# mLSTM and DSA stages of a three-block transformer kernel: score multiplies one step later, normalizations in pairs, mask and bias table summed on GpSimd

## The reference, cut to what matters

```python
# mLSTM, per head (the kernel does all 256 rows at once, the factors as one matrix exp(D))
s = einsum('blhd,bshd->bhls', q_, k_) * exp(D - m_t[..., None])
den = s.sum(-1) + ...
den = maximum(abs(den), exp(-m_t))
h = num / den.transpose(0, 2, 1)[..., None]
# DSA, per head
bias = rel_bias[t5_bucket(max(t - idx, 0))]
logits = (qb @ k_sel) * dh ** -0.5 + bias
logits = where(valid, logits, -inf)          # only the top-k keys of the indexer
probs = softmax(logits); out = probs @ v_sel
```

## Time and profile before

| | us |
|---|---|
| median of 3 runs | 882.55 (880.82 to 882.99) |
| the profiled execution | 882.83 |
| its span | 881.0 |
| granted clock of TensorE, mean | 0.996 of 2.4 GHz |

### The profile page before, as it was taken

How to read it: one execution, slowest core, us unless ns; L and a number is a source line. 1 busy time by engine, 2 the same in 40 slices (tenths; PEclk the granted TensorE clock), 3 DMA queues, 4 the chain that set the end, 5 groups by cost and what they waited for, 6 DMA issues and landing times. The chain is left out here.

```text
span 881.0 us, 14633 instructions
## 1 busy us (share of the span) xinstructions
PE 856.0 (97%) x5810; PEld 754.6 (86%) x5810; DVE 668.0 (76%) x1096; ACT 458.7 (52%) x737; POOL 66.2 (8%) x61
## 2 busy tenths in 40 slices
PE   9999989999999999999999999999999999999996
PEld 9989978767876888699999999679987899999995
DVE  6698798869977996799757857796777876556567
ACT  5564555454556645475454545265564854454450
POOL 1100001000001120011210100110000111001011
PEclk9999999999999999999999999999999999999999
DMA  9856576556965870799866897379617986645501
GB/s 344 298 178 200 191 245 226 191 157 206 337 238 206 276 272 1 304 371 374 288 221 218 290 342 251 118 242 351 226 50 277 330 294 203 210 153 196 187 1 48
DMA packets 56916, 200.67 MB, mean 228 GB/s; under 512 B 6600, under 2 KB 7936, under 8 KB 56848
## 3 DMA queue, kind: packets, MB, share of 16 engines
q1 hardware_dynamic: 55808, 196.50, 63.6%
q0 software_dynamic: 1040, 3.24, 1.2%
HBM read 198.57 MB, written 1.08 MB: 227 GB/s over the span
## 5 line engine op out<-in xcount | busy, mean ns | idle before, releaser
L1230 PE MATMUL ps<-XT,wsp 128*128 128x256 f32 x760 | 215.5, 283 | 2.2 <-DVE wsp L1471 1.3
L1231 PE MATMUL ps<-XT,wsp 128*128 128x256 f32 x760 | 212.5, 280 | 0.0
L1232 PE MATMUL ps<-XT,wsp 128*128 128x256 f32 x760 | 212.3, 279 | 0.0
L1471 DVE TENSOR_TENSOR wsp<-ring,wsp 128x1024 fp32r<-128x1024 f32 x140 | 173.5, 1248 | 7.5 <-ACT wsp L2047 7.3
L2047 ACT CAST wsp<-ring 128x1024 fp32r<-128x1024 f32 x140 | 145.5, 1046 | 61.6 <-PE ps L1232 52.8
L1230 PEld LDWEIGHTS ps<-XT,wsp 128*128 128x128 f32 x760 | 142.9, 188 | 5.9 <-issue 2.9
L1231 PEld LDWEIGHTS ps<-XT,wsp 128*128 128x128 f32 x760 | 142.8, 188 | 0.5
L1232 PEld LDWEIGHTS ps<-XT,wsp 128*128 128x128 f32 x760 | 142.7, 188 | 0.0
L1230 PE MATMUL ps<-wsp,ra 128*128 128x512 f32 (+1 forms) x256 | 97.6, 381 | 2.5 <-DVE ra L1508 1.1
L1232 PE MATMUL ps<-wsp,ra 128*128 128x512 f32 (+1 forms) x256 | 96.9, 379 | 0.0
L1231 PE MATMUL ps<-wsp,ra 128*128 128x512 f32 (+1 forms) x256 | 96.8, 378 | 0.0
(11 more groups left out here) (278 smaller groups left out, 1538.6 us busy)
## 6 DMA issues: line engine op xcount, KB each, us to landing
arena<-in_mod_w SPq DMA_DIRECT2D x48, 512.0 KB, 6.1
ring<-in_mod_w SPq DMA_DIRECT2D x44, 512.0 KB, 4.8
ring<-in_ffn_a SPq DMA_DIRECT2D x28, 512.0 KB, 5.0
ring<-in_ffn_b SPq DMA_DIRECT2D x28, 512.0 KB, 5.0
arena<-in_ffn_o SPq DMA_DIRECT2D x22, 512.0 KB, 4.7
ring<-in_ffn_o SPq DMA_DIRECT2D x22, 512.0 KB, 4.8
arena<-in_ffn_a SPq DMA_DIRECT2D x16, 512.0 KB, 5.4
arena<-in_ffn_b SPq DMA_DIRECT2D x16, 512.0 KB, 4.8
```

Of the source, the lines that this page charges most:

```text
L1230: pe.matmul(o, l[0], r[0], start=start, stop=False)
L1231: pe.matmul(o, l[0], r[1], start=False, stop=False)
L1232: return pe.matmul(o, l[1], r[0], start=False, stop=stop)
L1471: ve.tensor_tensor(w[:, 1024:1024 + n], raw[slot[0]][:, 0:n], w[:, 0:n].bitcast(f32), SUB).then_inc(*done("V", "lo", u, also=[("raw", *slo ...
```

## The change

- In `mlstm`, the second operation of a score tile becomes a step of its own, `ml_x`, queued one step of the mLSTM later: after `ml_s` of the next tile, and ahead of `ml_o`. The banks are given back there.
- The denominators: ScalarE takes Abs of the last column for each t (`ml_a`), and VectorE does maximum and reciprocal once per head, on two columns. ScalarE's scaling and squaring become a step `ml_h` behind both.
- In `dsa_steps`, `norm` becomes `norm2`, at even steps behind `sc`, for items i−2 and i−1: one reciprocal of two columns and two scalings. The remainder of `fin_dsa` becomes `fin_lo`, at the end of a step.
- The table products and `anti` are gone. The table is stored in reverse, and GpSimd adds mask and table into one of four buffers `bias` (`tbl`), two items ahead in the list; `sc` reads it in place of the mask.
- Some semaphores are merged (`GROUP`); a load into an area next to it waits for DSA's last reduction.

```diff
-        held = {}
+        held, late_x = {}, []
+        def ml_x():
+            h, j, b, s, b0 = late_x.pop(0)
+            add("ml_x", h, j, b, s, b0)
+            if j:
+                bank.put(b0[0])
+                bank.put(b[0])
         for h in range(5):
...
+                if late_x:
+                    ml_x()
+                if h < 4:
+                    late_x.append((h, j, b, s, bs[0]))
                 if h and j == 0:
-                    es = held.pop(h - 1)
+                    es, os = held.pop(h - 1), []
                     for t in range(2):
-                        b, s = bank.get(), pt.get()
-                        add("ml_o", h - 1, t, b, prior("bank", b), es, s, prior("pt", s))
-                        bank.put(b[0])
+                        os.append(bank.get())
+                        add("ml_o", h - 1, t, os[t], prior("bank", os[t]), es)
+                    for t in range(2):
+                        s = pt.get()
+                        add("ml_h", h - 1, t, os[t], s, prior("pt", s))
+                        bank.put(os[t][0])
                         pt.put(s[0])
...
+        add("tbl", 0)
+        add("tbl", 1)
         for i in range(n + lag + 2):
+            if i + 2 < n:
+                add("tbl", i + 2)
...
-            if 0 <= i - 1 < n:
-                add("norm", "dsa", i - 1, ps[i - 1])
+            if 1 < i <= n and i % 2 == 0:
+                add("norm2", i - 2, ps[i - 2], ps[i - 1])
+            if fins:
+                fin_lo()
             yield
...
-                        pe.matmul(ps[b[0]][:, 0:n], l, r, start=True, stop=False)
-                    for e_, b in enumerate(bs):
-                        for e in new("P", ("tb",), ("misc",)):
-                            pe.wait_ge(*e)
-                        pe.matmul(ps[b[0]][:, 0:n], anti, TB[:, of("dsa", i + e_)[0], 256 - n:256].bitcast(f32),
-                                  start=False, stop=True).then_inc(*done("P", "fill", *b))
+                        pe.matmul(ps[b[0]][:, 0:n], l, r, start=True, stop=True).then_inc(*done("P", "fill", *b))
...
+                elif kind == "ml_x":
+                    for e in new("V", ("ml_e", h, j, 1)):
+                        ve.wait_ge(*e)
                     ve.scalar_tensor_tensor(o, ps[b[0]][:, 256:256 + n], 0.25 * 128.0 ** -0.5, o, MUL, MUL).then_inc(
...
-                    ve.tensor_scalar(o, ps[b[0]][:, 256:257], -1.0, None, MUL).then_inc(*done("V", "ml_d", h, t, 0))
-                    ve.scalar_tensor_tensor(o, ps[b[0]][:, 256:257], em[:, t * 4 + h:t * 4 + h + 1], o, MAX,
-                                            MAX).then_inc(*done("V", "ml_d", h, t, 1))
-                    ve.reciprocal(o, o).then_inc(*done("V", "ml_d", h, t, 2))
+                    if t == 0:
+                        continue
+                    o, m_ = (grid(x, 2)[:, :, h] for x in (rdn, em))
+                    for e in new("V", ("ml_a", h, 1), ("ml_em",)):
+                        ve.wait_ge(*e)
+                    ve.tensor_tensor(o, o, m_, MAX).then_inc(*done("V", "ml_d", h, 0))
+                    ve.reciprocal(o, o).then_inc(*done("V", "ml_d", h, 1))
...
-                        for e in new("V", ("ix_sel", t), ("fill", *b), before):
+                        for e in new("V", ("tbl", i), ("fill", *b), before):
                             ve.wait_ge(*e)
-                        ve.tensor_tensor_reduce(p, ps[b[0]][:, 0:n], scr[:, (2 * t + 1) * 256:(2 * t + 1) * 256 + n],
-                                                -1.0, 3e38, ADD, MIN, nmx[:, i:i + 1]).then_inc(
+                        ve.tensor_tensor_reduce(p, ps[b[0]][:, 0:n], bias[i % 4][:, 0:n], -1.0, 3e38, ADD, MIN,
+                                                nmx[:, i:i + 1]).then_inc(
...
+                elif kind == "norm2":
+                    for e in new("V", ("exp", "dsa", i + 1)):
+                        ve.wait_ge(*e)
+                    ve.reciprocal(smx[:, i:i + 2], smx[:, i:i + 2]).then_inc(*done("V", "norm", "dsa", i, 0))
+                    for j in range(2):
+                        ve.tensor_scalar(p, p, smx[:, i + j:i + j + 1], None, MUL).then_inc(
+                            *done("V", "norm", "dsa", i + j, 1))
...
+                    ac.activation(rdn[:, t * 4 + h:t * 4 + h + 1], ps[b[0]][:, 256:257], ACT.Abs).then_inc(
+                        *done("A", "ml_a", h, t))
...
+                elif kind == "tbl":
+                    h, t = of("dsa", i)
+                    n = 128 * (t + 1)
+                    rel = bass.AP(ra, 6144 + h * 256 + n - 1, [[8192, 128], [-1, n]]).bitcast(f32)
+                    for e in new("G", ("ix_sel", 0), ("ix_sel", 1), ("tb",), ("nmx", "dsa", i - 4) if i > 3 else None):
+                        po.wait_ge(*e)
+                    po.tensor_tensor(bias[i % 4][:, 0:n], scr[:, (2 * t + 1) * 256:(2 * t + 1) * 256 + n], rel, ADD
+                                     ).then_inc(*done("G", "tbl", i))
```

More of the change, by code:

```diff
@@ L33 @@
 SIDE = 14
-MLSTM = ("ml_ac", "ml_em", "ml_e", "ml_d", "ml_h", "ml_sq", "ml_ms")
+MLSTM = ("ml_ac", "ml_em", "ml_e", "ml_d", "ml_a", "ml_h", "ml_sq", "ml_ms")
 TABLES = ("ang", "posf", "tab", "tab_k", "tab_r", "tab_c", "tab_sin", "dist", "dist_d")
+NORMS = ("rms1_sq", "rms1_ms", "rms1_rs", "rms1", "rms2_s", "rms2_m", "rms2_r", "rms2_x")
+GROUP = {k: name for name, kinds in (("tables", TABLES), ("mlstm", MLSTM), ("norms", NORMS)) for k in kinds}
 class Turn:
@@ L601, in mlstm @@
                 yield
-            for b in bs:
-                bank.put(b[0])
     W.finish(gts)
@@ L677, in dsa_steps, with fin_lo @@
                 bank.put(bs[i][0])
-            if 0 <= i - 1 < n:
-                add("norm", "dsa", i - 1, ps[i - 1])
+            if 1 < i <= n and i % 2 == 0:
+                add("norm2", i - 2, ps[i - 2], ps[i - 1])
+            if fins:
+                fin_lo()
             yield
+        while fins:
+            fin_lo()
+    fins = []
+    def fin_lo():
+        k, s = fins.pop(0)
+        add("fin_lo", k, s)
+        wk.put(s[0])
     def fin_dsa(k, b):
@@ L684, in fin_dsa @@
         add("fin_dsa", k, b, s, prior("wk", s))
-        wk.put(s[0])
+        fins.append((k, s))
     proj_b("u", 8, "w_az", 0, 4, lambda j, b: add("ev_az", j, b))
@@ L757, in before_gate @@
             free = [("gated", 1, 0), ("gated", 1, 1), ("tr", "hm1", 2)]
[L758 removed]
+            vs.append(Between(0, 2, [(SIDE, ("mod_one", 0, 3)), (SIDE + 2, ("nmx", "dsa", 15)), (SIDE + 7, ("fin_dsa", 3))] +
                               [(SIDE + 3 + n, free) for n in range(4)], 1, 2.0))
@@ L1113, in build @@
         wq = [mvf[:, i * 512:(i + 1) * 512] for i in range(4)]
-        anti, zero = scr[:, 1024:1152], scr[:, 1282:1410]
+        zero = scr[:, 1282:1410]
         gp = [ra[:, q * 1024:(q + 1) * 1024] for q in range(3)]
         TB = grid(ra[:, 6144:8192], 8)
+        bias = [arena[:, 7168 + i * 256:7424 + i * 256] for i in range(4)]
         def halves(t, off, n):
@@ L1204, in done @@
         def done(e, *key, also=(), by=1):
-            name = f"{'tables' if key[0] in TABLES else 'mlstm' if key[0] in MLSTM else key[0]}_{e}"
+            name = f"{GROUP.get(key[0], key[0])}_{e}"
             if name not in sems:
@@ L1381, in tensor @@
                 elif kind == "ml_o":
-                    h, t, b, before, es, s, _ = a
+                    h, t, b, before, es = a
                     for j in range(t + 1):
@@ L1777, in vector @@
                         *done("V", "fin_f", k, also=[("bank", *b)]))
+                elif kind == "fin_lo":
+                    k, s = a
+                    f = wk[s[0]][:, 0:256]
                     for e in new("V", ("fin_hi", k)):
@@ L2182, in scalar @@
                 elif kind == "ml_o":
-                    h, t, b, _, _, s, before = a
+                    h, t, b = a[0:3]
+                    for e in new("A", ("ml_o", h, t)):
+                        ac.wait_ge(*e)
+                    ac.activation(rdn[:, t * 4 + h:t * 4 + h + 1], ps[b[0]][:, 256:257], ACT.Abs).then_inc(
+                        *done("A", "ml_a", h, t))
+                elif kind == "ml_h":
+                    h, t, b, s, before = a
                     i = t * 4 + h
                     o = hm[:, i, :]
-                    for e in new("A", ("ml_d", h, t, 2)):
+                    for e in new("A", ("ml_d", h, 1)):
                         ac.wait_ge(*e)
@@ L2467, in sync @@
                     sp.dma_start(onehot, D["onehot"]).then_inc(*done("S", "misc", 3, by=16))
-                    sp.dma_start(anti, D["anti"]).then_inc(*done("S", "misc", 4, by=16))
                     sp.dma_start(grid(pT, 2), D["pT"].rearrange("(k p) n -> p k n", k=2)).then_inc(
```

21 lines of the change are left out of this document (12 added, 9 removed).

## The result

| | before | after |
|---|---|---|
| median, us | 882.52 (880.82 to 882.99) | 892.97 (892.39 to 894.73) |
| ratio | | 1.0125 [1.0105, 1.0146] |
| span of the profiled execution | 881.0 | 890.6 |
| mean granted clock | 0.996 | 0.987 |

The change made the kernel 10.4 us slower: 6.2 us above the forecast of 886.8 and 2 us above the end of its range. The direction was right, the size was not.

What follows compares the result with a forecast made beforehand. TensorE was taken to bound the kernel (busy 97%). From 882.8: −5.0 products, +3.0 mLSTM, +1.4 (4, 5), +2.3 (10, 11), +0.9 (16, 17), +1.7 clock = +4.3, so 887.1, against the median 886.8; range 878 to 891.

Steps and rivals of the forecast that it cites:

- mLSTM: mLSTM stage: deferred multiply makes TensorE wait before each head's last product, +4.2 us at head 3; net +3.0, bounds 0 to +4.
- The wait of 1.25 us at 123.42: mLSTM stage: TensorE's wait for a weight's low part, forecast to go because TensorE comes there 3 us later.
- The table products: DSA stage: two L1400 products fewer in each of 8 pairs, claimed as gain in full, −5.0 us.
- the wait in step 11: DSA, TensorE at head 8's transpose: waits for the scaling until 173.1, +4.2 us.
- (10, 11): DSA steps 10 and 11, run without weight product between: head 8's transpose waits for scaling, +4.2 us, net +2.3.
- The gated and the bank wait: DSA: TensorE's waits for gated tiles (0.5 us) and a bank (1.4 us), forecast to fall away in return.
- (16, 17): DSA steps 16 and 17: transpose waits behind `fin_dsa`, 0.34 + 0.19 + 0.35, so +0.9 us.
- (4, 5): DSA steps 4 and 5: transpose waits for reduction, reciprocal and scaling, with VectorE entering late; 1.4 us, of 0.9 to 3.
- Clock: Waits at head 3 (3.5 us) and step 11 (4.2 us): one fall counted, +1.7 us; two +3.4, none 0.
- two falls and GpSimd on the path: Rival: second fall 1.7 us, up to 1 us for each of two sums holding VectorE; 888.8 to 890.8, chance 0.20.
- It does what its name says: Rival: VectorE comes early enough that products and four waits go; 873.5, half about 878; chance 0.21 in full or half.
- The low parts: VectorE's low parts (two SBUF inputs) may each hold a GpSimd sum back or be held; no separate size given.

## Why the prediction was right in direction and wrong in size

**mLSTM: right.** I walked waits of 0.2, 1.5, 0.6 us and, for the last head, a multiply that ends at 120.1. The timeline of TensorE has none in front of head 0's and 1.18, 0.26 and 3.23 us in front of those of heads 1 to 3, and that of VectorE has the last multiply at 119.93:

```profile
115.43 0.41 DVE L1747 SCALAR_TENSOR_TENSOR pb<-ps,pb 128x256 f32<-128x256 f32 x1
115.76 1.28 DVE L1584 SCALAR_TENSOR_TENSOR R<-ring,cactr,R 128x1024 f32<-128x1024 f32 x1
...
119.93 0.28 DVE L1747 SCALAR_TENSOR_TENSOR pb<-ps,pb 128x128 f32<-128x128 f32 x1
```

The stage ends 4.2 us late, 1.7 of it clock: 2.5 against my +3.0. The wait of 1.25 us at 123.42 is gone, as said. One slip of mine is on record: 114.7 + 2.3 is 117.0 and not 116.7, so that the wait of 3.5 us that I gave for the clock should have been 3.1; it measured 3.23.

**The table products: right in the changed kernel, "in full" wrong as a reason.** I wrote that TensorE has no wait there but those named, so the gain is full. With the products alone taken out, 5.0 became 2.7. A chain without slack counts like a wait that is not there yet. In the sum for the changed kernel this cost nothing, since the wait in step 11 was counted from TensorE's earlier arrival.

**(10, 11): the right transpose, 4.2 against 5.8.** It is item 8's, TensorE stands from about 174.6, and the scaling releases it. Two things were taken at zero. GpSimd's sum holds the scaling: "on the chain of (10, 11) it costs 0 to 1; I take 0". And VectorE enters the gating operations late: 173.75 against 166.95 is +6.8 where TensorE is +5.8. The run without sums takes 1.06 us off the wait, and its trace parts the two. From the start of the scaling to the transpose it is 180.42 − 179.59 = 0.83 us in after and 175.30 − 174.96 = 0.34 there, so the held scaling is 0.5. From the start of the gating to that of step 10's scores it is 173.93 − 173.75 = 0.18 us in after, 169.87 − 169.12 = 0.75 there and 168.15 − 166.95 = 1.20 in before: 0.6 of VectorE's lag is GpSimd's too, and 0.45 stays without it. In VectorE's timeline of after:

```profile
173.75 0.69 DVE L1840 SCALAR_TENSOR_TENSOR wk<-wk,ps 128x512 f32<-128x512 f32 x1 [0.85 <-ACT wk L2297]
...
179.59 0.97 DVE L1809 TENSOR_SCALAR pb<-pb,small 128x128 f32<-128x128 f32 x2
```

The gated and the bank wait fell away as said, and (16, 17) came to 0.73 against 0.9.

**(4, 5): 1.4 against 3.1.** The cause I named, GpSimd's first sum behind the power operation, was right; its size was not. I let VectorE lose 1.3 us, and then, choosing "1.4, of 0.9 to 3", gave only 0.5 of that to the wait. Moving four sums forward took 1.45 us off it. VectorE had next to no idle time in between to make the delay good, and beside sums its own operations took longer (0.58 for two scalings became 1.27, 1.28 for a modulation step 1.76):

```profile
144.88 0.29 DVE L1776 CUSTOM_DVE_ANT_0 pb<-ps,arena 128x128 f32<-128x128 f32 x1 [1.35 <-POOL arena L2452]
...
149.01 1.27 DVE L1809 TENSOR_SCALAR pb<-pb,small 128x128 f32<-128x128 f32 x2
...
154.01 1.76 DVE L1584 SCALAR_TENSOR_TENSOR R<-ring,cactr,R 128x1024 f32<-128x1024 f32 x1
```

**Clock: the step that failed most.** "I count one fall, +1.7", with two for a rival. There were three, worth 5.2 us by the run with spare products: that is 3.5 of the 6 us that the forecast missed, with 1.8 from (4, 5) and 1.3 from (10, 11), less 0.5 at mLSTM. My own row already asked for two: before 328 us TensorE was busy 0.86 of 2 us, and the waits of mLSTM and (10, 11), which I put at 3.5 and 4.2 us, leave it idler than that; I gave no reason for charging only one. The third stood behind (4, 5), whose wait I had put at 1.4 us: at 3.1 us it came, at 1.67 us (sums early) it came still, at 0.85 us (no sums) it didn't. I also took the price of a fall from a single place. Every wait above what before shows harmless should have been charged with a fall, at least in the range.

**The sum, mended:** −5.0 + 2.5 + 3.2 + (6.0 − 0.9 − 1.5) + 0.9 + 5.2 = +10.4 (waits, and in the brackets the gated and the bank wait of before that fell away, as start-to-start excess), against +10.0 in TensorE's timeline. Of the rivals "two falls and GpSimd on the path" (888.8 to 890.8) named all of the mechanisms and was still 2 us short, for the third fall. "It does what its name says" came true only with the readers moved (876.9 to 878): in after VectorE reaches head 3's multiply at 119.93, no sooner than it reached that place in before.

## What to carry to other kernels

An operation that is deferred by a step takes the step out of its reader's slack; move the reader with it, or the queue in between becomes the wait. The same edit was worth +10.4 us without and −4 us with two readers moved; which of the two mattered more in the full change is not shown. Where an engine is freed of work, look for the chains that were just on time in before, for they are the next bound. And in a TensorE bound kernel price a new wait of a few us at its length and something for the clock: here 5.2 us on 12.1, an estimate from three waits of one trace; in two other traces the fall behind the same wait of mLSTM cost 0.8 and 1.2 us more.

## What the runs showed of the hardware

**Sums on GpSimd lengthen VectorE's scaling.** Groups of the stage from 138 to 205 us, VectorE in before and in the run with mLSTM's reader later (single scaling in both), then GpSimd's sums there:

```profile
L1770 DVE TENSOR_SCALAR pb<-pb,small 128x256 f32<-128x256 f32 x8 | 2.8, 354 | 0.3
...
L1770 DVE TENSOR_SCALAR pb<-pb,small 128x128 f32<-128x128 f32 x8 | 2.3, 287 | 0.3
```

```profile
L1798 DVE TENSOR_SCALAR pb<-pb,small 128x256 f32<-128x256 f32 x8 | 4.8, 600 | 0.3
...
L1798 DVE TENSOR_SCALAR pb<-pb,small 128x128 f32<-128x128 f32 x8 | 3.9, 492 | 0.3
```

```profile
L2452 POOL TENSOR_TENSOR arena<-arena,ra 128x256 f32<-128x256 f32 x8 | 7.9, 986 | 14.9 <-DVE small L1776 14.9
L2452 POOL TENSOR_TENSOR arena<-arena,ra 128x128 f32<-128x128 f32 x8 | 3.6, 465 | 7.1 <-DVE small L1776 7.1
```

A scaling costs 0.2 us more on the average, and it stands on the chain that TensorE waits for. The control is the run without sums, which has the pairs and everything else of after: there (130 to 205 us) they take what they took in before.

```profile
L1805 DVE TENSOR_SCALAR pb<-pb,small 128x256 f32<-128x256 f32 x8 | 2.5, 351 | 0.1
L1805 DVE TENSOR_SCALAR pb<-pb,small 128x128 f32<-128x128 f32 x8 | 1.9, 284 | 0.1
```

A sum starts the moment the maximum frees its buffer, which is just when the reciprocal and the scaling follow: the dependency brings the two together. The low parts, which I had feared for, stayed at 1220 ns in after against 1219 in before, and their group of 11 at 1271 in the run with mLSTM's reader later. But a sum that meets one is long: the sum of 256 columns at 153.03 in after, beside a low part of 1.22 us that started at 152.87, took 1.66 us, where one at 145.66 in the run with mLSTM's reader later took 0.74. The Trainium skill, "SBUF — State Buffer", section "Who interferes with whom", names `tensor_scalar` as an operation that can take the pair of ports it shares with GpSimd; by that rule, the trace agrees, I should have charged the scaling.

**The clock fell behind shorter waits than I had thought.** Waits of 1.19 and 1.44 us in before left it alone; behind one of 1.67 us (sums early, TensorE busy 0.42 of the 2 us up to 156) it was granted at 0.63 and 0.52. Near 325 to 340 us the same work, with TensorE busy 0.86 of 2 us in before, was followed by a fall in before and after and by none in the run with fitted spare products. The Trainium skill, "TensorE: Matmul & The Clock Gate", section "Why this matters for your kernels", puts the limit at gaps of about 3 us; here the clock fell behind a gap of 1.67 us, and the measurement decides.

**The clock makes much of the spread between executions.** The 18 executions of before on the chip of the last four runs sort by their mean granted clock: 880.6 to 881.2 us at 0.998, 881.9 to 882.8 at 0.996, 884.0 and 884.1 at 0.994. And one fall isn't like another: behind mLSTM's wait of 3.2 us, the same in all three, after lost 1.7 us by its windows and the runs with single normalization and with the sums early 3.4 each (DSA's first scores start at 144.23 and 143.87 there, at 143.03 in after). A gain of 1 to 2 us in a single execution may be nothing but this.
